# Weight sums from VectorE to GpSimd, and loads and side work in another order, in the gate stage of a hybrid decoder step

## What is computed

```
h = rms_norm(x) * (1 + scale) + shift
q, k, v, z_a, u_b, z_b, g_a, g_b = split(h @ w_in)
a = softmax-weighted sum over 3 groups of dilated attention (prompt and samples)
p = pooling branch of u_b
ya = (a * silu(z_a)) @ w_a_out
yb = (p * silu(z_b)) @ w_b_out
m  = sigmoid(g_a) * ya + sigmoid(g_b) * yb
y  = x + gate * (m @ w_out)
```

## Time and profile before

| | us |
|---|---|
| median of 3 runs | 2184.86 (2183.28 to 2186.05) |
| the profiled execution | 2182.39 |
| its span | 2180.6 |
| TensorE busy | 2079.2 |
| VectorE busy | 1090.7 |
| ScalarE busy | 689.0 |
| GpSimd busy | 338.7 |
| mean granted TensorE clock | 0.987 of full |

### The profile page before, as it was taken

One profiled execution on the slowest core, in us unless ns is written; L12 is line 12 of the kernel. 1 busy time (PEld: TensorE's weight loads), 2 busy tenths in 40 slices (PEclk: granted clock), 3 DMA queues, 4 the chain that ended last, 5 costly groups with the idle time before them and its releaser, 6 DMA issues.

```text
span 2180.6 us, 38700 instructions
## 1 busy us (share of the span) xinstructions
PE 2079.2 (95%) x13575; PEld 1977.1 (91%) x13575; DVE 1090.7 (50%) x2691; ACT 689.0 (32%) x2278; POOL 338.7 (16%) x453
## 2 busy tenths in 40 slices
PE   5999999999999999999999999899969987999999
PEld 3889999999999999999999999899958976998887
DVE  3543333334434444343422455487757757666664
ACT  4633333333333333333361111333333332111010
POOL 2222112112111111121105565000000000000000
PEclk9999999999999999999999999999989999999999
DMA  9756675664555646554336653678955564544432
GB/s 348 246 178 198 206 223 191 202 203 152 185 171 174 197 144 198 169 166 146 93 97 202 192 202 129 207 192 204 265 164 155 144 198 159 187 153 144 145 128 61
DMA packets 292924, 387.96 MB, mean 178 GB/s; under 512 B 26212, under 2 KB 251828, under 8 KB 291341
## 3 DMA queue, kind: packets, MB, share of 16 engines
q1 hardware_dynamic: 237945, 343.48, 49.9%
q10 hardware_dynamic: 54812, 42.33, 6.8%
HBM read 277.54 MB, written 196.40 MB: 217 GB/s over the span
## 4 chain that ended last, share of the span: by engine, by line
PE 85%; DVE 5%; DMA 3%; SPq 2%; issue 2%; ACT 2%; POOL 1%; ACTq 0%; DVEq 0%
PE a_pp L1081 12%; PE a_pp L1079 12%; PE a_pp L1080 12%; PE g_bank L1079 4%; PE g_bank L1081 4%; PE g_bank L1080 4%; PE pp L1079 3%; PE pp L1081 3%; PE pp L1080 3%; PE c_py L1079 3%; PE c_py L1081 3%; PE c_pa L1080 3%; PE c_pa L1081 3%; PE c_py L1080 3%; PE c_pa L1079 3%
## 5 line engine op out<-in xcount | busy, mean ns | idle before, releaser
L1079 PE MATMUL a_pp<-a_wH,hH 128*128 128x384 f32 x1520 | 527.2, 347 | 5.8 <-DVE qkv L1721 5.2
L1081 PE MATMUL a_pp<-a_wH,hL 128*128 128x384 f32 x1520 | 514.8, 339 | 0.0
L1080 PE MATMUL a_pp<-a_wL,hH 128*128 128x384 f32 x1520 | 513.0, 338 | 0.0
L1710 DVE TENSOR_SCALAR a_ms<-a_ss 128x2 f32<-128x2 f32 (+1 forms) x204 | 34.4, 169 | 520.9 <-ACT a_junk L1599 520.8
L1079 PEld LDWEIGHTS a_pp<-a_wH,hH 128*128 128x128 f32 x1520 | 286.0, 188 | 9.7 <-ACT qkv L1605 4.4
L1079 PE MATMUL g_bank<-hH,aH 128*128 128x258 f32 x896 | 260.4, 291 | 27.8 <-DVE hL L665 21.4
L1080 PEld LDWEIGHTS a_pp<-a_wL,hH 128*128 128x128 f32 x1520 | 286.3, 188 | 0.0
L1081 PEld LDWEIGHTS a_pp<-a_wH,hL 128*128 128x128 f32 x1520 | 285.3, 188 | 0.0
L1599 ACT ACTIVATE a_junk<-a_pp 128x128 f32<-128x128 f32 x384 | 106.6, 278 | 540.9 <-PE a_pp L1081 534.7
L1507 POOL TENSOR_TENSOR a_rs<-a_ms,a_mhalf 128x2 f32<-128x2 f32 (+1 forms) x204 | 140.9, 691 | 838.2 <-DVE a_ms L1710 838.2
L1081 PE MATMUL g_bank<-hH,aL 128*128 128x258 f32 x896 | 257.7, 288 | 0.0
(11 more groups left out here) (290 smaller groups left out, 3939.5 us busy)
## 6 DMA issues: line engine op xcount, KB each, us to landing
out_dram<-in_state_kv_w_dram SPq DMA_DIRECT2D x64, 1023.5 KB, 5.6
qkv_dram<-qkv SPq DMA_DIRECT2D x192, 192.0 KB, 2.1
qkv_in<-qkv_dram SPq DMA_DIRECT2D x192, 192.0 KB, 2.6
a_wst<-in_w_in_dram SPq DMA_DIRECT2D x38, 512.0 KB, 7.2
gl<-gT_dram SPq DMA_DIRECT2D x64, 264.0 KB, 3.9
gT_dram<-out ACTq DMA_DIRECT2D x64, 257.0 KB, 6.2
w<-in_w_in_dram SPq DMA_DIRECT2D x64, 256.0 KB, 6.4
out_dram<-in_state_kv_w_dram SPq DMA_DIRECT2D x8, 2044.0 KB, 11.2
```

The lines of the kernel that those rows point to most:

```text
L1079: nc.tensor.matmul(out, sH, mH, start=(i == 0), stop=False)
L1080: nc.tensor.matmul(out, sH, mL, start=False, stop=False)
L1081: last = nc.tensor.matmul(out, sL, mH, start=False, stop=(i == len(terms) - 1))
L1710: nc.vector.tensor_scalar(ms[0:rows, s % 2, :], ss[0:rows, s % 2, :], 1.0 / E, EPS, ALU.mult, ALU.add).then_inc(meaned, 1)
```

## The change

- `weight_sums` is issued by GpSimd, for all 16 steps in a row, each waiting for its loads and for the low parts of the step before; VectorE's queue loses it. `token_lo(0, 5)` comes one product earlier.
- SP: the weights of step 1 are loaded ahead of the keys of sample 0, those of step 9 among the installs in iteration 7 (three ahead of install 4, one ahead of install 6). The last shifted copy moves from iteration 7 to 10; `load_weights(0)` from 8 to 9; values 2 to 7 are spread over iterations 9 to 12. The combine inputs (zl, bl) and the first four gate pairs (gl) are loaded in iteration 14, ahead of the last step's weight pieces.
- Values are weighed after products 0 and 3 (was 0 and 2) and summed before products 3 and 6 (was 3 and 5).
- The first group difference and exponential of both tiles come after product 2 of step 14, the rest of the sums after product 3 and after product 0 of step 15 (was: all of tile 0 after product 0, of tile 1 after product 5 of step 14). `sum_groups` is cut in two functions for this.
- Weight piece 3 of the combination is split in step 15, and the pieces 4 to 7 at other branches. Tiles bl, zl, gl and abL change places.

```
-                def gate_weights(s):
+                def gate_weights(s, blocks=range(4)):
...
+                gate_weights(1)
                 keys(0)
...
-                        if s + 1 < GS:
+                        if s + 1 < GS and s not in (0, GP):
                             gate_weights(s + 1)
                         if s + 1 < NS:
                             keys(s + 1)
-                        if s < NS:
-                            shifted_copy(sp, v, 0, s, bulk)
+                        if s < NS - 1 or s == GP + 2:
+                            shifted_copy(sp, v, 0, min(s, NS - 1), bulk)
...
                             for i in range(1, NP):
+                                if i == 4:
+                                    gate_weights(GP + 1, range(3))
+                                if i == 6:
+                                    gate_weights(GP + 1, (3,))
                                 sp.wait_ge(g_done, NP * s + i)
                                 install(1, i)
...
-                            sp.wait_ge(g_done, NP * GP)
-                            load_weights(0)
                             sp.wait_ge(p_ready, 2)
...
-                        if GP + 2 <= s < GP + 5:
-                            for b in range(2):
-                                values(2 * (s - GP - 1) + b)
+                        if s == GP + 1:
+                            sp.wait_ge(g_done, NP * GP)
+                            load_weights(0)
+                        for b in {GP + 1: (2,), GP + 2: (3,), GP + 3: (4, 5), GP + 4: (6, 7)}.get(s, ()):
+                            values(b)
...
-                        if s == GS - 1:
+                        if s == GS - 2:
                             for i in range(2):
                                 sp.wait_ge(b_stored[i], 16 * PAIRS * NBC // 2)
-                            sp.wait_ge(g_lo, NP * GS)
                             branch_inputs(0)
+                            for i in range(4):
+                                sp.wait_ge(g_stored[i], 16 * GP)
+                            gates(0, range(4))
+                        if s == GS - 1:
                             for n, freed in enumerate((0, 2, 4, 5, 1, 3, 6), 1):
                                 sp.wait_ge(g_done, NP * s + freed + 1)
                                 load_weights(n)
-                                if n == 2:
-                                    for i in range(4):
-                                        sp.wait_ge(g_stored[i], 16 * GP)
-                                    gates(0, range(4))
...
+                def weight_sums(s):
+
+                    pool.wait_ge(g_landed, 64 * (s + 1))
+                    if s:
+                        pool.wait_ge(g_lo, NP * s)
+                    nc.gpsimd.tensor_tensor(w4[:, 4, :, :], w4[:, 2, :, :], w4[:, 3, :, :], ALU.add).then_inc(g_sum, 1)
+                    pool.wait_ge(g_sum, 4 * s + 1)
+                    nc.gpsimd.tensor_tensor(w4[:, 2, :, :], w4[:, 0, :, :], w4[:, 2, :, :], ALU.subtract).then_inc(g_sum, 1)
+                    nc.gpsimd.tensor_tensor(w4[:, 5, :, :], w4[:, 4, :, :], w4[:, 0, :, :], ALU.subtract).then_inc(g_sum, 1)
+                    pool.wait_ge(g_sum, 4 * s + 3)
+                    nc.gpsimd.tensor_tensor(w4[:, 6, :, :], w4[:, 1, :, :], w4[:, 5, :, :], ALU.subtract).then_inc(g_sum, 1)
...
+                for s in range(GS):
+                    weight_sums(s)
...
-                            if i == 1 and s + 1 < GS:
-                                weight_sums(s + 1)
+                            if s == 0 and i == 1:
+                                token_lo(0, 5)
                             for n in READY_AT.get(i, ()) if s + 1 < GS else ():
                                 weight_lo(s + 1, n)
-                            if s == 0 and i == 2:
-                                token_lo(0, 5)
...
-                            if s == GP + 1 and i == 2:
+                            if s == GP + 1 and i == 3:
                                 weigh(0)
-                            if GP + 2 <= s < GP + 5 and i in (0, 2):
-                                weigh(2 * (s - GP - 2) + i // 2 + 1)
+                            if GP + 2 <= s < GP + 5 and i in (0, 3):
+                                weigh(2 * (s - GP - 2) + i // 3 + 1)
...
-                            if s == GS - 2 and i in (0, 5):
-                                n = i // 5
-                                dve.wait_ge(ol_landed[n], 16)
-                                sum_groups(nc, ol[n][:, :, :], cw[:, n], chained, ol_diff, lambda: dve.wait_ge(ol_exp, n + 1)).then_inc(a_ready, 1)
+                            if s == GS - 2 and i == 2:
+                                for n in range(2):
+                                    dve.wait_ge(ol_landed[n], 16)
+                                    group_diff(nc, ol[n][:, :, :], cw[:, n], chained, ol_diff)
+                            if s == GS - 2 and i == 3:
+                                dve.wait_ge(ol_exp, 1)
+                                group_rest(nc, ol[0][:, :, :], cw[:, 0], chained).then_inc(a_ready, 1)
+                            if s == GS - 1 and i == 0:
+                                dve.wait_ge(ol_exp, 2)
+                                group_rest(nc, ol[1][:, :, :], cw[:, 1], chained).then_inc(a_ready, 1)
...
-                                if i == 5:
-                                    weights_lo(2)
+                                if i >= 5:
+                                    weights_lo(i - 3)
...
-                            if s == GS - 2 and i in (0, 5):
-                                group_exp(i // 5)
+                            if s == GS - 2 and i == 2:
+                                for n in range(2):
+                                    group_exp(n)
                             if s == GS - 1:
-                                if i == 2:
+                                if i == 1:
                                     pooling_hi()
...
+                                if i == 6:
+                                    weights_hi(3)
...
-                            if s == GP + 1 and i == 5:
+                            if s == GP + 1 and i == 6:
                                 values(0)
-                            if GP + 2 <= s < GP + 5 and i in (3, 5):
-                                values(2 * (s - GP - 2) + (i - 3) // 2 + 1)
+                            if GP + 2 <= s < GP + 5 and i in (3, 6):
+                                values(2 * (s - GP - 2) + (i - 3) // 3 + 1)
...
-        LATE_HI, LATE_LO = {0: 3, 1: 4, 2: 5, 4: 6, 6: 7}, {0: 3, 2: 4, 4: 5, 6: 6, KT - 1: 7}
+        LATE_HI, LATE_LO = {0: 4, 2: 5, 3: 6, 5: 7}, {1: 4, 3: 5, 5: 6, KT - 1: 7}
```

More of the change, by code:

```diff
@@ L388, in values @@
                         sp.dma_start(vt[b % 2][g][:, :], carried(g, b, 1)).then_inc(v_landed[b % 2][g], 16)
-                def gate_weights(s):
+                def gate_weights(s, blocks=range(4)):
                     f = s % GP
-                    for i, (c0, kh) in enumerate(((CGA, K1), (CGA, K2), (CGB, K1), (CGB, K2))):
+                    for i in blocks:
+                        c0, kh = ((CGA, K1), (CGA, K2), (CGB, K1), (CGB, K2))[i]
                         if s:
@@ L1048, in sum_groups, with group_diff, group_rest @@
 def sum_groups(nc, o, cw, chained, diff_ready, wait_exp):
-    m, l = o[:, :, E + 1:E + 2].rearrange("p n o -> p (n o)"), o[:, :, E:E + 1].rearrange("p n o -> p (n o)")
+    group_diff(nc, o, cw, chained, diff_ready)
+    wait_exp()
+    return group_rest(nc, o, cw, chained)
+def group_diff(nc, o, cw, chained, diff_ready):
+    m = o[:, :, E + 1:E + 2].rearrange("p n o -> p (n o)")
+    by_head = m.rearrange("p (g h) -> p h g", h=HEADS)
+    as_groups = lambda ap: ap.rearrange("p (g h) -> p g h", h=HEADS)
+    chained(nc.vector.tensor_reduce(cw[:, 0, 0:HEADS], by_head, AX.X, ALU.max))
+    nc.vector.tensor_tensor(as_groups(cw[:, 1, :]), as_groups(m), cw[:, 0, 0:HEADS].unsqueeze(1).to_broadcast([P, GROUPS, HEADS]),
+                            ALU.subtract).then_inc(diff_ready, 1)
+def group_rest(nc, o, cw, chained):
+    l = o[:, :, E:E + 1].rearrange("p n o -> p (n o)")
     by_head = lambda ap: ap.rearrange("p (g h) -> p h g", h=HEADS)
@@ L1054, in sum_groups @@
     row = lambda k: cw[:, k, :]
-    chained(nc.vector.tensor_reduce(row(0)[:, 0:HEADS], by_head(m), AX.X, ALU.max))
-    nc.vector.tensor_tensor(as_groups(row(1)), as_groups(m), over(row(0)[:, 0:HEADS]), ALU.subtract).then_inc(diff_ready, 1)
-    wait_exp()
     chained(nc.vector.tensor_tensor(row(3), row(2), l, ALU.mult))
@@ L2029, in combine @@
         abH = sb("abH", [P, KT, CS], F32R)
-        abL = sb("abL", [P, KT, CS], F32R)
-        gl = [sb(f"gl{i}", [P, 2, CS]) for i in range(RG)]
         bl = sb("bl", [P, 4, CS])
         zl = sb("zl", [P, 4, CW])
+        sb("pad1", [P, 32])
+        gl = [sb(f"gl{i}", [P, 2, CS]) for i in range(RG)]
+        abL = sb("abL", [P, KT, CS], F32R)
         a32 = sb("a32", [P, 4, CS])
```

13 lines of the change are left out of this document (1 added, 12 removed).

## The result

The changed kernel takes 2174.45 us (median of 5 runs, 2171.88 to 2176.61) against 2186.05 of the kernel before on the same chip (5 runs): ratio 0.995, 95% interval 0.9936 to 0.9964. That is 11.6 us between the medians and 10.9 by the ratio. A second pair on another chip gave 0.9947 (0.9934 to 0.996). The forecast was 2164 us, a gain of 21: the time lies in its range of 2147 to 2180, and the gain is about half of it.

A forecast was written before the change was run, and what follows sets the result against it. TensorE bounds the kernel (busy 2079.2 of 2180.6 us), so gains come from its idle 101. Terms 6.5 - 2.5 + 6.5 - 1.7 + 0.9 + 1.5 + 10 = 21.2 take 2182.39 to 2161.2; plus 2.5 for the median, 2164; range 2147 to 2180.

The forecast's parts named there:

- GpSimd's undisturbed duration: Weight sums on GpSimd: 1.10 or 1.30 us each undisturbed, four taken as 4.9 us, against 2.8 on VectorE.
- Step 0: gains 6.5: Step 0: weights 1 issued ahead of keys 0, so 5.5 us lost instead of 12.0; bounds 9.7 and 4.
- Steps 2 to 6: loses 2.5: Steps 2 to 6: GpSimd's longer chain makes product 3's sum 0.5 us late in five steps; bounds 0 and 8.
- Steps 7 and 8: gains 6.5: Steps 7 and 8: weights 9 among the installs land at about 1587, not 1595.65; bounds 0 and 14.
- Step 9: loses 1.7: Step 9: weights 10 still late, values 0 need the whole chain; 32.9 us against 31.2; bounds +2 and -4.
- Steps 10 to 13: gains 0.9: Steps 10 to 13: moving the second weighing to product 3 takes away about 1.2 us in step 10; bounds +2 and -3.
- Steps 14 and 15: gains 1.5: Steps 14 and 15: later first part, but step 15 loses waits; 52.7 us instead of 54.2; bounds -2 and +6.
- Entrance: gains 10: Entrance of the combination: shorter queue and earlier splits, last product to branch 4 14.7 us instead of 22.8; bounds 5 and 12.
- if the last gate store lands as late as now: Entrance of the combination: one of three stated conditions under which the forecast fails; VectorE's wait was expected about 8.5 us, not 12.2.
- Rival C: Transfers hidden no better than before: steps 7 and 8 give nothing, entrance 4; 12.5 us more, 2176 us; chance 0.17.
- Rival A: GpSimd and VectorE block each other, four sums about 10 us; steps 2 to 7 cost 30 more, 2194 us; chance 0.1.

The follow-up runs named there:

- experiment 2: Kernel before with only the new steps 14 and 15 preparation and combination entrance: 0.9952. Kernel after with only those undone: 1.0001.
- experiment 5: Kernel after, weights 10, 15 forward, values 2 behind weights 11: 0.9856 (sums on GpSimd), 0.9844 (VectorE); copies moved too: 0.9847, 0.978; copies behind values: 0.9836, 0.9773.
- experiment 6: The combination on VectorE plus four unused 512-column GpSimd additions in each of steps 0 to 12: 0.99 of the kernel before, 26 us above the same without them.
- the combination: Kernel after (sums on GpSimd) with weights 10 and 15 put forward, values 2 behind weights 11, copies in steps 9 to 12: 0.9847 of the kernel before.
- the combination on VectorE: The combination with the weight sums on VectorE instead of GpSimd: 0.978 of the kernel before, 48.1 us below it.

## Where the prediction failed, and what was right

The direction, the places and GpSimd's undisturbed duration were right; the sum of 21.2 us was twice what came. The step that failed is the sum over steps 0 to 13, 6.5 - 2.5 + 6.5 - 1.7 + 0.9 = 9.7 us, which measured 0 (experiment 2; 0.3 by the table). Its gravest fault is that it has no term for step 1, which lost 4.7 us; step 9 fell short by 2.6 and steps 10 to 13 by 2.1. Outside it the entrance fell short by 3.6. Those four are 13.0 us, against 12.6 missing by the profiles.

- **Step 0: gains 6.5.** It gained 5.2. The first score starts at 1408.17, 3.9 us later than before instead of 2.5, two scores take 1.8 us each beside GpSimd's sums, and product 4 waits 2.8 us instead of 1.5. The larger fault is that the account stopped at the step's end. Step 1 isn't in the sum and lost 4.7 (6.3 in the first profile). Before, weights 2 were issued in the time that step 0 lost; without it they land 12.7 or 9.2 us into step 1. Late transfers and GpSimd's chain both stretch it: with the sums on VectorE and the copies in place step 1 still takes 26.1 us, with GpSimd and the copies moved 22.4 to 23.7, with VectorE and the copies moved 20.2. How the 4.7 us divide isn't settled.
- **Steps 2 to 6: loses 2.5.** Measured 0.8, with profiles that scatter by 2. The price was the longer chain less what the earlier keys relieve, and the text had both. It is a price of this order of loads only: 2.4 us in the changed kernel, 8 to 15 once the loads land early (experiment 5).
- **Steps 7 and 8: gains 6.5.** Measured 6.1; weights 9 landed at 1590.8 instead of the predicted 1587, and 2.3 us earlier in the second profile. Alone the move gives 9.6.
- **Step 9: loses 1.7.** Lost 4.3. The weights landed 15.2 us in instead of 14.0, so VectorE's first low part started 21.2 us in instead of some 19.5: 1.2 by the landing, 0.5 by sums and high part, 6.0 us where the text had 5.5. The values' matmul came at 28.1 (text: 27.5), and product 6 behind the idle took 5.0 us (text: 4.2; the granted clock of this window is 0.80). The chain was right, each link a little short.
- **Steps 10 to 13: gains 0.9.** Lost 1.2. The sentence that "keys, values and the copy pass no queue but SP's, whose waits there (on values already used) are the same as before" is wrong: values 2 moved ahead of weights 11 and brought their wait with them, and weights 11 land at 8.2 instead of 4.6 us. Undoing it alone brought the landing back to 5.6 us and left the step at 26.1, so this fault alone didn't set the loss. With VectorE's sums step 10 takes 27.2 us where weights 11 land late (8.7) and 23.5 where they land at 5.1 to 6.4; with GpSimd's it takes 25.6 to 27.4 for landings from 5.0 to 8.8, and 30.7 for 11.4. Two causes, each enough alone: the late weights and GpSimd's sums, which meet the combination of the new rows.
- **Steps 14 and 15: gains 1.5.** Measured 1.9, step 15 starting 29.6 and 30.0 us in as predicted. With VectorE's sums (experiment 2) it is 3.7: GpSimd's share is about 2.
- **Entrance: gains 10.** Measured 6.4. The text named its own test, "if the last gate store lands as late as now", and it does: VectorE passes the wait 12.3 us behind the last product instead of 8.5. The store is issued 3.3 us behind that product and lands 8.7 us later, and the change moves neither. From the wait to branch 4 it takes 6.3 us, as forecast (6.2; before 10.7): that gain of 4.4 came, and the 2.2 before the first output product.

Rival C (transfers no better hidden, 2176 us) was nearest in number, but not in cause: steps 7 and 8 gave what was forecast. Rival A's blocking happened little with these loads (10 of the 56 sums from step 1 on take over 1.4 us, 1.74 at most), since VectorE mostly stood idle at that point, as the text argued; the added GpSimd work of experiment 6 shows its price where it does. The rule of the Trainium skill (SBUF — State Buffer, Who interferes with whom), by which the second waits out the first, agrees with those rows but for some 0.3 us: the added addition takes 1.04 us alone and VectorE's sum 0.69, together 1.73, and a pair takes 1.45; in step 10 above, 1.28 and 0.68 are 1.96, and a pair takes 1.70.

The version that beats both is the changed kernel with the sums left on VectorE, weights 10 and 15 put forward, values 2 behind weights 11 and the copies in steps 9 to 12 or 10 to 13: 0.978 and 0.9773 of the kernel before, 48 to 50 us faster.

## What to carry to other kernels

When a stall is taken away, ask what was fetched during it: follow the loads of the next step, from what frees their room to their landing, before the gain is booked. Price moving work to another engine by the chain from the landing data to the first consumer, in every step, and price it again once loads have been reordered: here it was some 2 us, within noise, with the loads as they were, and 8 to 15 once they came early. In a queue that is written out by hand, the cheapest gains are loads that stand behind a wait that they don't need: moving two of them, with values 2 put back, gave 20.6 us.

## What the runs showed of the hardware

Work on GpSimd slows even tiny operations of VectorE. In step 9 of the combination, beside GpSimd's sums, VectorE's scaling of 32x384 took 1.34 us and that of 32x3 elements 1.23 (first rows, then GpSimd's); in the combination on VectorE they take 0.41 and 0.21 (last rows).

```profile
1605.24 1.34 DVE L759 TENSOR_SCALAR pcr<-pcr,st 32x384 f32<-32x384 f32 x1
1606.51 1.23 DVE L760 TENSOR_SCALAR pcn<-pcn,st 32x3 f32<-32x3 f32 x1
```

```profile
1605.11 1.26 POOL L562 TENSOR_TENSOR w<-w 128x512 f32<-128x512 f32 x1 [14.77 <-DVE aL L682]
1606.45 1.27 POOL L564 TENSOR_TENSOR w<-w 128x512 f32<-128x512 f32 x1
```

```profile
1599.42 0.41 DVE L760 TENSOR_SCALAR pcr<-pcr,st 32x384 f32<-32x384 f32 x1
1599.76 0.21 DVE L761 TENSOR_SCALAR pcn<-pcn,st 32x3 f32<-32x3 f32 x1
```

Each loses 0.9 to 1.0 us, and so do L778 and L779 above, whatever their own size. That is no fixed price but the rest of the GpSimd sum that they met: the two scalings end at 1606.58 and 1607.74, the GpSimd sums at 1606.37 and 1607.72. Beside the shorter additions of experiment 6 (1.04 us) the same two take 1.10 and 1.00. A single weight tile of 256 KB, issued alone into queues that held a copy and gate stores, took 11.5 us to land in the kernel after (weights 2, the last tile, issued at 1424.03, landed at 1435.48).
